# Eight instead of six projection units ahead of the recurrence, and eight instead of ten ahead of the state-space part

## The chip, the cores and the metric

The kernel runs on one core of one Trainium2 chip. A core has five engines that run their own instruction streams and meet through semaphores: TensorE (PE in the rows; PEld is its weight load), VectorE (DVE), ScalarE (ACT), GpSimd (POOL) and SyncE (SP, which here only issues DMAs). The metric is the device time of one execution in microseconds. The kernel before takes 3821.53 us, the median of three runs from 3819.82 to 3821.96.

## The reference, cut to what matters

The program computes two transformer-like blocks in a row. The change lies in the second block, in its mixers. There a normed input h (1024 tokens x 1024 channels) is projected by one wide weight, and four mixers work on slices of the result:

```
h = rmsnorm_2(x, g_mix[l])
u = h @ w_in[l]
c_q, c_kv, k_r, u_pool, z, xbc, dt, lru_g, lru_x, gates = jnp.split(u, pts, axis=-1)
y_a = mla_mixer(...)     # attention
y_b = pool_mixer(u_pool, ...)
y_c = ssd_mixer(z, xbc, dt, ...)     # state-space part: silu(causal conv(xbc)), then chunks
y_d = rglru_mixer(lru_g, lru_x, ...) # recurrence: causal conv, two gates, scan, gelu gate
```

Each mixer needs only its own columns of u; the gates are needed after all four. So the projection can be made piece by piece, in between the mixers' own work.

## The kernel before, in words

`mixers` (L3452) builds one block in which every engine runs one long list: the join of the first block's result (`Join`), then the recurrence (`Recurrence`), the pooling mixer (`Pooling`), the state-space part (`StateSpace`), attention (`Attention`), and what is left of the projection.

The projection (`Projection`, F in the code) has 60 weight tiles of 128 columns, n = 0 to 59, and each tile gives two units, m = 2n and 2n + 1, one for each half of the 1024 tokens. A unit is 24 matmuls of 128x512 (8 steps over the channels, each as three products of split values, lines L100 to L102). Its output bank is one of three, by m modulo 3. Tiles 0 to 7 are, in turn, the x and g parts of the recurrence's four channel groups; 8 to 11 are the pooling's, 12 to 17 the convolution inputs of the state-space part, 18 holds dt and the rotary key, 19 to 22 are z.

A tile takes this way. SP loads it (`load`, L2611). POOL splits it into a high and a low part (`halve`, L2622 and L2624) into one of two buffers. PE makes its two units (`multiply`). ACT copies each unit out of its bank (`take`, L2671), the even unit of a tile only after the store of the tile two before has landed. SP stores the tile to a scratch in HBM (`store`, L2677). The mixer that wants it has SP load it from there (`lr_x`, `lr_g`, `po_u`, `sda_x`).

Nothing is planned by a scheduler: the order on each engine is the order of the calls. `multiply(pe, count)` on PE and `take(act, count)` on ACT make the next `count` units wherever they stand, and both keep a running number, so a call with a larger count shifts every later unit forward. The first three units are made inside the join, so that `multiply(pe, 6)` ahead of the recurrence adds units 3, 4 and 5.

ACT runs `F.take(act, lru.FIRST)` and then `lru.scalar`, whose first work is the exponential and logarithm of a small table sp8 (L2815, L2817). DVE's list of the recurrence waits for those two (`act_own`) before its first convolution (L2723 to L2726, then the bias, L2778). PE's first recurrence matmuls (L2808) wait for that convolution. After them come, for each of four channel groups, 4, 4, 4 and 2 units. Pooling has 4 units first, then one behind each of its four matmul pairs (L2895). The state-space part then has 10 units before its first own work on PE, and two after that.

SP's list is one loop over the tiles. In turn n it issues the load of tile n + 2, the store of tile n, and whatever loads the mixers want of tile n. In turn 12 the state-space part's loads begin, and they begin with a wait for the end of the recurrence and the pooling (L2911 is the pooling's):

```
if n == U_XBC:
    for e in self.earlier:
        e.over(sp)
```

`over` waits until all stores of that mixer have landed. Tile 14 is issued in turn 12 ahead of this wait, tile 15 in turn 13 behind it.

Of the kernel before, what the change touches and what calls it, by code (L numbers as in the profile page):

```python
# [348 lines left out]
class Inputs:  # L349
# [163 lines left out]
    def turn(self, pe, bank, ident):  # L513
        x = self.turns
        i = self.rows[x]
        n, a, m, last = self.pieces[i]
        pe.wait_ge(self.taken, i + 1)
        if x >= 2:
            pe.wait_ge(self.placed, x - 1)
        for c in range(m // P):  # L520
            mm = self.nc.tensor.transpose(bank[:, c * P:(c + 1) * P], self.ob[self.slot[i]][:, c * P:(c + 1) * P], ident)
        mm.then_inc(self.turned, 1)
        self.turns += 1
# [2205 lines left out]
class Recurrence:  # L2729


    FIRST, NEXT = 6, (4, 4, 4, 2)

    def __init__(self, nc, s, q, A, R, F, banks):
        self.nc, self.A, self.R, self.F, self.ps = nc, A, R, F, banks
# [178 lines left out]
class StateSpace:  # L2914
# [114 lines left out]
    def tensor(self, pe):  # L3029
        mm_, ps, C = self.nc.tensor.matmul, self.ps, self.C  # L3030
        turn = self.nc.tensor.transpose
        self.F.multiply(pe, 10)
        for e in self.earlier:
            e.over(pe)
        pe.wait_ge(self.got, 96)
        pe.wait_ge(self.dt_in, 16)
        for c in range(NCK):
            mm = turn(ps[4][:, c * SH:(c + 1) * SH], self.dtr[:, c * P:(c + 1) * P], C["ident"][0:SH, 0:SH])
        mm.then_inc(self.d_turned, 1)
        self.F.multiply(pe, 2)  # L3040
        pe.wait_ge(self.ready, 2)
        mm_(ps[4][:, 0:NCK * SH], self.incl[:], self.a[:].rearrange("p c h -> p (c h)"), start=True, stop=True)
        mm_(ps[4][:, BANK // 2:BANK // 2 + NCK * SH], C["ones"][:], self.a[:].rearrange("p c h -> p (c h)"), start=True, stop=True).then_inc(self.summed, 1)
        pe.wait_ge(self.silu, 6)
        for i in range(NCK):
            if i >= 2:
                pe.wait_ge(self.moved, i - 1)
            for n in range(4):
                turn(ps[i % 2][:, n * P:(n + 1) * P], self.xo[:, n, i * P:(i + 1) * P], C["ident"][:])
            mm = turn(ps[2 + i % 2][:, 0:P], self.xo[:, 4, i * P:(i + 1) * P], C["ident"][:])  # L3050
            mm.then_inc(self.turned, 1)
            if i % 4 == 3:
                self.F.multiply(pe, 1)

        def rows(i):
            r = [slice(0, 64), slice(64, P)]
            mm_(ps[2][:, 0:P], self.xo[r[0], 4, i * P:(i + 1) * P], self.xo[r[0], 5, i * P:(i + 1) * P], start=True, stop=True).then_inc(self.first, 1)
            for h in range(SH):
                mm_(ps[h // 4][:, h % 4 * P:(h % 4 + 1) * P], self.a[:, i, h:h + 1].broadcast_to([P, P]), self.incl[:], start=True, stop=True)
            pe.wait_ge(self.first, i + 1)  # L3060
            mm_(ps[2][:, P:2 * P], self.xo[r[1], 4, i * P:(i + 1) * P], self.xo[r[1], 5, i * P:(i + 1) * P], start=True, stop=True).then_inc(self.rowed, 1)

        pe.wait_ge(self.moved, NCK)
        rows(0)
        for i in range(NCK):
            pe.wait_ge(self.y_done, i)
            pe.wait_ge(self.y_full, i)
            pe.wait_ge(self.xb_done, i + 1)
            r = [slice(0, 64), slice(64, P)]
            mm_(ps[3][:, 0:256], self.xo[r[0], 5, i * P:(i + 1) * P], self.S[r[0], 0:256], start=True, stop=True).then_inc(self.begun, 1)  # L3070
            mm_(ps[4][:], self.bt[:, i], self.xb[i % 2][:], start=True, stop=True).then_inc(self.summed, 1)
            pe.wait_ge(self.begun, i + 1)
            mm_(ps[3][:, 256:512], self.xo[r[1], 5, i * P:(i + 1) * P], self.S[r[1], 256:512], start=True, stop=True).then_inc(self.summed, 1)
            pe.wait_ge(self.masked, 2 * i + 2)
            if i + 1 < NCK:
                rows(i + 1)
            self.F.halves(pe, 1)
            pe.wait_ge(self.y_done, i + 1)
            for h in range(SH):
                mm = mm_(ps[3][:, h * SHD:(h + 1) * SHD], self.M[:, h, :], self.xt[:, i, h * SHD:(h + 1) * SHD], start=True, stop=True)  # L3080
            mm.then_inc(self.summed, 1)
            self.F.halves(pe, 1)
        self.F.settle()
        self.F.multiply(pe, 1)
        pe.wait_ge(self.z_silu, 4)
        for i in range(NCK):
            if i >= 2:
                pe.wait_ge(self.gated, i - 1)
            for n in range(4):
                mm = turn(ps[i % 2][:, n * P:(n + 1) * P], self.z[:, n, i * P:(i + 1) * P], C["ident"][:])  # L3090
            mm.then_inc(self.z_turned, 1)
        self.F.multiply(pe, 3)
        for i in range(NCK):
            pe.wait_ge(self.scaled, i + 1)
            if i >= 2:
                pe.wait_ge(self.o_moved, i - 1)
            for n in range(4):
                mm = turn(ps[2 + i % 2][:, n * P:(n + 1) * P], self.y[:, i, n * P:(n + 1) * P], C["ident"][:])
            mm.then_inc(self.o_turned, 1)
            if i % 4 == 3:  # L3100
                self.F.multiply(pe, 1)

    def scalar(self, act):
        S, ps = self.nc.scalar, self.ps
        for e in self.earlier:
            e.over(act)
        act.wait_ge(self.got, 96)
        for n in range(6):
            self.F.take(act, 1 if n < 2 else 2)
            act.wait_ge(self.convd, n + 1)  # L3110
            S.activation(self.xo[:, n, :], self.xo[:, n, :], ACT.Silu, bias=self.cb[:, n:n + 1]).then_inc(self.silu, 1)
        S.activation(self.al[:], self.al[:], ACT.Exp).then_inc(self.exped, 1)
        act.wait_ge(self.ready, 1)
        S.activation(self.u[:], self.u[:], ACT.Exp).then_inc(self.exped, 1)
        act.wait_ge(self.exped, 2)
        S.activation(self.u[:], self.u[:], ACT.Ln, bias=1.0).then_inc(self.exped, 1)
        self.F.take(act, 2)
        for i in range(NCK):
            act.wait_ge(self.turned, i + 1)
            S.activation(self.xt[:, i], ps[i % 2][:], ACT.Copy)  # L3120
            S.activation(self.bt[:, i], ps[2 + i % 2][:, 0:P], ACT.Copy).then_inc(self.moved, 1)
            if i % 4 == 3:
                self.F.take(act, 1)
        act.wait_ge(self.ready, 3)
        S.activation(self.eacs[:], self.acs[:], ACT.Exp).then_inc(self.exped, 1)
        S.activation(self.back[:], self.back[:], ACT.Exp).then_inc(self.exped, 1)
        S.activation(self.tot[:], self.tot[:], ACT.Exp).then_inc(self.exped, 1)
        for i in range(NCK):
            act.wait_ge(self.lready, i + 1)
            S.activation(self.L[i % 2][:], self.L[i % 2][:], ACT.Exp).then_inc(self.lexped, 1)  # L3130
            if i:
                self.F.take(act, 1)
        self.F.take(act, 1)
        act.wait_ge(self.z_in, 64)
        for n in range(4):
            S.activation(self.z[:, n, :], self.z[:, n, :], ACT.Silu).then_inc(self.z_silu, 1)
        self.F.take(act, 1)
        for i in range(NCK):
            act.wait_ge(self.gated, i + 1)
            S.activation(self.M[:].rearrange("p h t -> p (h t)")[:, i % 2 * BANK:(i % 2 + 1) * BANK], self.y[:, i], ACT.Square, accum_out=self.ms[:, i:i + 1]).then_inc(self.squared, 1)  # L3140
            if i % 2:
                act.wait_ge(self.squared, i + 1)
        self.F.take(act, 3)
        act.wait_ge(self.gated, NCK + 1)
        S.activation(self.ms[:], self.ms[:], ACT.Sqrt).then_inc(self.rooted, 1)
        for i in range(NCK):
            act.wait_ge(self.o_turned, i + 1)
            for n in range(4):
                ins = S.activation(self.yT[:, n, i * P:(i + 1) * P], ps[2 + i % 2][:, n * P:(n + 1) * P], ACT.Copy, scale=self.gn[:, n:n + 1])
            ins.then_inc(self.o_moved, 1)  # L3150
            if i % 4 == 3:
                self.F.take(act, 1)
        act.wait_ge(self.o_moved, NCK)
        act.dma_start(self.R["y"][8:12].rearrange("k p t -> p k t"), self.yT[:, 0:4, :]).then_inc(self.stored, 16)
# [502 lines left out]
class Tail:  # L3657
# [7 lines left out]
    NB, PAIRS, FIRST = 7, 16, 16  # L3665
# [972 lines left out]
```

## Time and profile before

| | |
|---|---|
| median of three runs | 3821.53 us (3819.82 to 3821.96) |
| the profiled execution | 3822.48 us |
| its span | 3820.8 us |
| PE busy | 3473.8 us, 91% |
| DVE busy | 2424.8 us, 63% |
| ACT busy | 1581.6 us, 41% |
| POOL busy | 1121.3 us, 29% |

The span is the time from the first to the last instruction in the profile of one execution; the 1.7 us beside it lie around it. A share is an average over the whole program, and the program has many stages: what an edit does is read from its own stage, which here lies between 1700 and 1960 us of the span.

### The profile page before, as it was taken

Reading aid. Unit: us, or ns where it says so; the run is one execution under the profiler, and the core shown is the slowest. Engines: PE = TensorE matmul, PEld = TensorE weight load, DVE = VectorE, ACT = ScalarE, POOL = GpSimd, SP = SyncE. Lnnn points to the kernel's source line nnn. Section 1 sums busy time; section 2 is a strip of 40 time slices with the busy share of each in tenths; the row PEclk is TensorE's granted clock in tenths of the full one; section 3 lists DMA queues with packets and bytes.
Section 4 is the critical chain, followed back from the end, with each engine's and each line's share of the span. In section 5 each row is a group of like instructions: output and inputs, shape, how many; then the busy total and the mean of one; then the engine's idle time right before and its main releaser. Section 6 shows DMA issues by size and latency. Waiting matters only on the chain. (4 is left out here: it accounts for less than half of the span.)

```text
span 3820.8 us, 44308 instructions
## 1 busy us (share of the span) xinstructions
PE 3473.8 (91%) x16308; PEld 2772.4 (73%) x16308; DVE 2424.8 (63%) x2813; ACT 1581.6 (41%) x2197; POOL 1121.3 (29%) x675
## 2 busy tenths in 40 slices
PE   7899988595999999968989899999889889999997
PEld 3678777464888888846677667777777678878876
DVE  5569557646888888866656222222246488877778
ACT  4322234444777777734221222222232342234444
POOL 1232220135111111143331212222143455545442
PEclk9899999796999999989999999999999999999999
DMA  5312246646899999954421311111153524478854
GB/s 191 110 50 82 104 143 216 223 156 255 354 404 406 404 403 407 393 193 145 156 105 56 127 47 67 59 67 63 55 210 132 190 96 154 153 275 279 266 169 138
DMA packets 225015, 716.70 MB, mean 188 GB/s; under 512 B 26832, under 2 KB 61488, under 8 KB 208720
## 3 DMA queue, kind: packets, MB, share of 16 engines
q1 hardware_dynamic: 184000, 620.37, 44.6%
q10 hardware_dynamic: 31056, 64.28, 4.5%
q0 software_dynamic: 9792, 29.81, 2.0%
q8 instruction: 106, 1.74, 0.2%
q14 instruction: 61, 0.50, 0.0%
HBM read 573.48 MB, written 140.89 MB: 187 GB/s over the span
## 5 line engine op out<-in xcount | busy, mean ns | idle before, releaser
L100 PE MATMUL m_b<-b_high,m_high 128*128 128x512 f32 x960 | 403.5, 420 | 7.7 <-POOL m_low L2624 6.6
L102 PE MATMUL m_b<-b_high,m_low 128*128 128x512 f32 x960 | 377.0, 393 | 0.0
L101 PE MATMUL m_b<-b_rest,m_high 128*128 128x512 f32 x960 | 376.5, 392 | 0.0
L2622 POOL TENSOR_TENSOR m_high<-m_raw,m_one 128x1024 fp32r<-128x1024 f32 x60 | 119.7, 1995 | 759.8 <-PE m_b L102 681.8
L3918 POOL TENSOR_TENSOR t_wl<-t_buf,t_wh 128x512 fp32r<-128x512 f32 x136 | 194.9, 1438 | 240.7 <-ACT t_wh L4049 240.6
L100 PE MATMUL zs_z<-zs_hs,zs_high 128*128 128x512 f32 (+1 forms) x584 | 228.1, 391 | 8.8 <-DVE zs_hs L310 8.3
L2671 ACT ACTIVATE m_ob<-m_b 128x512 f32<-128x512 f32 x120 | 71.0, 596 | 374.3 <-PE m_b L102 338.2
L100 PE MATMUL t_b<-b_high,t_wh 128*128 128x512 f32 x544 | 215.1, 395 | 10.9 <-POOL t_wl L3918 10.9
L100 PEld LDWEIGHTS m_b<-b_high,m_high 128*128 128x128 f32 x960 | 182.2, 190 | 56.0 <-issue 10.2
L101 PE MATMUL zs_z<-zs_hs,zs_high 128*128 128x512 f32 (+1 forms) x584 | 220.3, 377 | 0.0
L102 PE MATMUL zs_z<-zs_hs,zs_low 128*128 128x512 f32 (+1 forms) x584 | 220.3, 377 | 0.0
L101 PEld LDWEIGHTS m_b<-b_rest,m_high 128*128 128x128 f32 x960 | 182.3, 190 | 45.0 <-issue 8.1
L101 PE MATMUL t_b<-b_rest,t_wh 128*128 128x512 f32 x544 | 213.2, 392 | 0.0
L102 PE MATMUL t_b<-b_high,t_wl 128*128 128x512 f32 x544 | 213.0, 391 | 0.0
L2248 DVE TENSOR_TENSOR ex_wlo<-moe_raw,ex_who 128x2048 fp32r<-128x2048 f32 x78 | 178.7, 2293 | 50.4 <-ACT ex_who L2194 49.7
L102 PEld LDWEIGHTS m_b<-b_high,m_low 128*128 128x128 f32 x960 | 181.6, 189 | 39.4
L2248 DVE TENSOR_TENSOR ex_wlg<-ex_raw,ex_whg 128x2048 fp32r<-128x2048 f32 x78 | 178.8, 2293 | 42.0 <-ACT ex_whg L2194 41.8
L4049 ACT ACTIVATE t_wh<-t_buf 128x512 fp32r<-128x512 f32 x136 | 85.8, 631 | 262.0 <-PE t_b L102 77.6
L2248 DVE TENSOR_TENSOR ex_wlu<-moe_raw,ex_whu 128x2048 fp32r<-128x2048 f32 x78 | 178.1, 2284 | 4.0 <-ACT ex_whu L2194 4.0
L428 POOL TENSOR_TENSOR zs_high<-zs_raw,zs_one 128x1024 fp32r<-128x1024 f32 x29 | 58.9, 2030 | 413.7 <-PE zs_z L102 408.5
L3442 DVE TENSOR_SCALAR at_o<-m_b,at_sm 128x64 f32<-128x64 f32 x64 | 18.2, 284 | 228.9 <-PE m_b L3272 201.8
L2194 ACT ACTIVATE ex_whu<-moe_raw 128x2048 fp32r<-128x2048 f32 x78 | 149.4, 1918 | 28.9 <-PE ex_pu L102 26.0
(707 smaller groups left out, 9467.7 us busy)
## 6 DMA issues: line engine op xcount, KB each, us to landing
moe_raw<-in_expert_w SPq DMA_DIRECT2D x79, 2048.0 KB, 10.2
ex_raw<-in_expert_w SPq DMA_DIRECT2D x39, 2048.0 KB, 10.5
t_raw<-in_w_ff SPq DMA_DIRECT2D x192, 256.0 KB, 3.6
m_raw<-in_w_ug SPq DMA_DIRECT2D x60, 512.0 KB, 4.4
t_buf<-hid SPq DMA_DIRECT2D x112, 256.0 KB, 4.4
hid<-t_x SPq DMA_DIRECT2D x96, 256.0 KB, 2.3
yrows<-ex_y ACTq DMA_DIRECT2D x38, 512.0 KB, 10.7
gates<-m_ob SPq DMA_DIRECT2D x32, 512.0 KB, 2.8
```

What stands on the lines that cost most here:

```text
L100: nc.tensor.matmul(out, w[0], x[0], start=first, stop=False)
L101: nc.tensor.matmul(out, w[0], x[1], start=False, stop=False)
L102: return nc.tensor.matmul(out, w[1], x[0], start=False, stop=last)
L428: g.tensor_tensor(self.high[j][:], self.raw[j][:], self.one[:].broadcast_to([P, D]), ALU.mult).then_inc(self.rounded, 1)
L2194: S.activation(half(wh[u], x_), half(raw[slot], x_), ACT.Copy).then_inc(rounded, 1)
L2248: V.tensor_tensor(half(wl[u], x_), half(raw[slot], x_), half(wh[u], x_).bitcast(F32), ALU.subtract).then_inc(left, 1)
L2622: g.tensor_tensor(W.high[j][:], W.raw[j][:], W.one[:].broadcast_to([P, D]), ALU.mult).then_inc(W.rounded, 1)
L2671: self.nc.scalar.activation(self.ob[n % 2][:, c * BANK:(c + 1) * BANK], self.banks[m % len(self.banks)][:], ACT.Copy).then_inc(self.taken, 1)
L3442: V.tensor_scalar(self.o[p % 2][:, b, h % 2 * VH:(h % 2 + 1) * VH], ps[4][:, n % 2 * P:n % 2 * P + VH], sm[:, 1:2], None, ALU.mult).then_i ...
L3918: G.tensor_tensor(self.wl[:, f % 4], self.source(f), self.wh[:, f % 4].bitcast(F32), ALU.subtract).then_inc(self.split, 1)
L4049: S.activation(self.wh[:, f % 4], self.source(f), ACT.Copy).then_inc(self.rounded, 1)
```

## The change

`Recurrence.FIRST` goes from 6 to 8 (PE and ACT both use it), `StateSpace.tensor` multiplies 8 units in front in place of 10, and `StateSpace.scalar` takes one unit ahead of each of its first four activations in place of the first two, so that it takes 8 there in place of 10.

```
-    FIRST, NEXT = 6, (4, 4, 4, 2)
+    FIRST, NEXT = 8, (4, 4, 4, 2)
...
     def tensor(self, pe):
         mm_, ps, C = self.nc.tensor.matmul, self.ps, self.C
         turn = self.nc.tensor.transpose
-        self.F.multiply(pe, 10)
+        self.F.multiply(pe, 8)
...
         for n in range(6):
-            self.F.take(act, 1 if n < 2 else 2)
+            self.F.take(act, 1 if n < 4 else 2)
```

Units 6 and 7 move in front of the recurrence. All units from 8 to 29 are made one place of two earlier in the lists; from unit 30 on each stands where it stood.

## Rows read from the trace of the kernel before

**Rows 1.** Window: length, busy PE, PEld, DVE, ACT, POOL, PE clock, DMA share, GB/s.
```profile
1740.60:1890.00 149.40, 146.80 (x586) 111.46 (x587) 100.58 (x77) 66.50 (x80) 54.25 (x22) 0.97 0.38 139
```

**Rows 2.** Timeline of PE: start, us, instruction, count [idle before, releaser].
```profile
1729.76 0.39 PE L102 MATMUL m_b<-b_high,m_low 128*128 128x512 f32 x1
...
1740.61 3.78 PE L2808 MATMUL m_b<-lr_xc,lr_wa 128*128 128x512 f32 x4 [10.47 <-DVE lr_xc L2778]
...
1871.80 3.43 PE L2895 MATMUL m_b<-po_d,po_w 128*128 128x512 f32 x4 [2.59 <-DVE po_d L2886]
...
1880.55 1.99 PE L2895 MATMUL m_b<-po_d,po_w 128*128 128x512 f32 x4
...
1905.47 0.79 PE L100 MATMUL m_b<-b_high,m_high 128*128 128x512 f32 x1 [6.58 <-POOL m_low L2624]
```

**Rows 3.** Timeline of ACT ahead of the recurrence, and two later takes.
```profile
1730.22 1.09 ACT L2671 ACTIVATE m_ob<-m_b 128x512 f32<-128x512 f32 x2 [10.32 <-DMA u<-m_ob]
...
1734.14 0.20 ACT L2817 ACTIVATE lr_sp<-lr_sp 128x4 f32<-128x4 f32 x1
...
1929.15 0.60 ACT L2671 ACTIVATE m_ob<-m_b 128x512 f32<-128x512 f32 x1 [4.84 <-PE m_b L102]
...
1940.03 0.60 ACT L2671 ACTIVATE m_ob<-m_b 128x512 f32<-128x512 f32 x1 [4.84 <-PE m_b L102]
```

**Rows 4.** Timeline of DVE: the recurrence's first convolution.
```profile
1734.45 0.17 DVE L2770 TENSOR_SCALAR lr_lam<-lr_lam 128x4 f32<-128x4 f32 x1 [5.53 <-ACT lr_sp L2817]
...
1739.81 0.75 DVE L2778 TENSOR_SCALAR lr_xc<-lr_xc,lr_cb 128x1024 f32<-128x1024 f32 x1
```

**Rows 5.** Timeline of SP's DMA issues.
```profile
1735.82 0.32 SPq L2756 DMA_DIRECT2D lr_g<-u  x1
1736.18 0.43 SPq L2611 DMA_DIRECT2D m_raw<-in_w_ug  x1
...
1743.06 0.43 SPq L2611 DMA_DIRECT2D m_raw<-in_w_ug  x1
...
1893.97 0.43 SPq L2611 DMA_DIRECT2D m_raw<-in_w_ug  x1
```

**Rows 6.** Timeline of POOL: splits of tiles 3, 4, 14 and 15.
```profile
1721.41 2.40 POOL L2624 TENSOR_TENSOR m_low<-m_raw,m_high 128x1024 fp32r<-128x1024 f32 x1
1741.51 1.89 POOL L2622 TENSOR_TENSOR m_high<-m_raw,m_one 128x1024 fp32r<-128x1024 f32 x1 [17.70 <-DMA m_raw<-in_w_ug]
...
1869.38 2.12 POOL L2622 TENSOR_TENSOR m_high<-m_raw,m_one 128x1024 fp32r<-128x1024 f32 x1 [10.04 <-PE m_b L102]
...
1900.16 1.98 POOL L2622 TENSOR_TENSOR m_high<-m_raw,m_one 128x1024 fp32r<-128x1024 f32 x1 [26.20 <-DMA m_raw<-in_w_ug]
1902.22 3.20 POOL L2624 TENSOR_TENSOR m_low<-m_raw,m_high 128x1024 fp32r<-128x1024 f32 x1
```

**Rows 7.** Timeline of DVE: steps of pooling and convolutions, beside a split and alone.
```profile
1853.62 0.18 DVE L2885 TENSOR_TENSOR po_d<-lr_x,po_inv 128x16 f32<-128x16 f32 x1
...
1864.75 1.23 DVE L2882 TENSOR_TENSOR lr_x<-po_u 128x1024 f32<-128x1024 f32 x1 [10.74 <-DMA y<-po_d]
...
1869.79 1.75 DVE L2885 TENSOR_TENSOR po_d<-lr_x,po_inv 128x16 f32<-128x16 f32 x1
...
1871.98 3.06 DVE L2882 TENSOR_TENSOR lr_x<-po_u 128x1024 f32<-128x1024 f32 x1 [0.23 <-DMA y<-po_d]
...
1903.25 3.25 DVE L2726 SCALAR_TENSOR_TENSOR sd_xo<-sda_x,sd_cw,sd_xo 128x1024 f32<-128x1024 f32 x1
...
1939.42 1.29 DVE L2726 SCALAR_TENSOR_TENSOR sd_xo<-sda_x,sd_cw,sd_xo 128x1024 f32<-128x1024 f32 x1
```

**Rows 8.** Waits of SP's DMA queue, 1700 to 1960: us in total, times, longest.
```profile
SPq L2911 <- DMA y<-po_d: 20.5, 1, 20.5
```

**Rows 9.** Windows as in rows 1, after the two idle times of PE.
```profile
1744.00:1746.00 2.00, 2.00 (x6) 0.81 (x4) 0.00 (x0) 1.01 (x2) 1.83 (x1) 0.74 0.86 332
...
1908.00:1910.00 2.00, 2.00 (x8) 1.59 (x8) 1.97 (x2) 0.16 (x1) 1.92 (x2) 0.78 0.51 209
```

## The prediction

> **What bounds the kernel now.** I read the busy time by engine first: PE has the largest share, but a share of the whole says nothing of a stage, so I went to windows of the stage that the change touches. Between 1740.6 and 1890 us PE is busy for 146.80 of 149.40 us [rows 1]; the idle time lies ahead of that stretch and behind it. The timeline of PE names the three holes. 10.47 us before the recurrence's first matmuls, ended by DVE's convolution. 2.59 us in pooling, ended by DVE. 6.58 us before 1905.47, ended by POOL's split of a weight tile [rows 2]. So PE's own work bounds the middle, and two chains of other engines bound its two ends. What counts is how the start of unit 30 moves: from there on all lists are as they were, with the same units in the same places, so a shift there reaches the end of the kernel whole.
>
> **The first hole, and what the two units do to it.** Unit 5 ends at 1729.76 + 0.39 = 1730.15 [rows 2]. Units 6 and 7 can follow at once: tile 3 is split by 1721.41 + 2.40 = 1723.8 [rows 6], unit 6's bank was emptied before (ACT's takes of units 0 to 3 lie before the wait in rows 3), and unit 7's bank is free once unit 4 is taken, at about 1730.8 [rows 3]. A unit is (1940.03 - 1929.15) / 2 = 5.44 us [rows 3]. So they run from 1730.15 to 1741.03, in the place of the hole.
>
> But the hole was not free time of the recurrence; it was the time of a chain. ACT takes units 4 and 5 (1730.22, 1.09 for both), then runs the exponential and the logarithm until 1734.34. DVE waits for that, convolves from 1734.45 to 1740.56, and PE goes on at 1740.61 [rows 2 to 4]. From the last take to PE that is 1740.61 - 1731.31 = 9.3 us. In the changed kernel ACT has two more takes ahead of the same chain, and the last needs unit 7. It starts at about 1741.1 and ends at 1741.7, where it ended at 1731.31: +10.4 us. The take of unit 6 also wants the store of tile 1 landed; SP's load of that tile, which waits for the same landing, goes out at 1735.82 [rows 5], 0.2 us after unit 6 is ready (1735.6), and unit 7 covers that. PE's hole is thus moved behind the two units, not filled. Term one: **+10.4**.
>
> **A split that now falls on the convolution.** Tile 4 is loaded at 1736.18 and its split starts when it lands, 1741.51, 5.3 us later. Tile 5 is loaded at 1743.06 [rows 5, 6]. Before, its split had to wait for PE to leave tile 3, until after the recurrence's first matmuls; now PE leaves tile 3 at 1741.03, so the split starts at landing, 1743.06 + 5.3 = 1748.4. The convolution now runs from 1744.9 to 1751.0 and meets it. What a DVE step loses to each of the two POOL instructions stands in rows: beside the subtraction (POOL from 1902.22) a convolution step takes 3.25 us and alone 1.29, so 1.96; beside the multiplication (POOL from 1869.38) a small step takes 1.75 and alone 0.18, so 1.57 [rows 6, 7]. Together 3.5. At 1748.4 the last 2.6 us of the convolution are left, enough for both to come between steps. The bounds are 0 (the tile lands after 1751.0) and 4.3 (DVE stands for both in full, 1.89 and 2.40 us). I take the 3.5 of the rows, as the tile would have to land over 2 us late to miss. Term two: **+3.5**.
>
> The Trainium skill, "SBUF — State Buffer", section "Who interferes with whom", says that DVE and GpSimd hold their shared ports for a whole instruction and that the other then blocks entirely. The step of 3.25 us agrees. By that rule both POOL instructions would stand in front of a DVE step here in full, and the sum would end 0.8 higher.
>
> **The middle.** The recurrence and the first part of pooling keep 14 and 8 units, the same matmuls, and the same order; PE has 97% of a full clock there [rows 1] and hardly a hole, so they cost the same. Scratch loads of the recurrence come a tile earlier, but no PE hole there is put down to one, so I count nothing (bounds -1 and +1: one convolution ends within 1 us of when PE wants it).
>
> In pooling one thing changes. Splits are triggered when PE leaves a tile, so the split at 1869.38 (tile 14) would now be that of tile 15, which is not loaded yet (below). It was in DVE's way: a step of 16 columns took 1.75 in place of 0.18 us, and the next group's first step 3.06 in place of 1.23 [rows 7]. Without it pooling's third matmuls start 1.6 us earlier (1870.2). The fourth wait for DVE, which starts at 1871.98 because of a store, and ends 1.8 us earlier, at 1878.7, in place of 1880.5 [rows 2, 7]. PE is ready about then. Bounds: 0, and 3.3 if the lost clock of the 2.59 us hole came back whole as well. Term three: **-1.8**.
>
> **The last hole, and why nothing comes back there.** The two units taken off the state-space front are units 28 and 29 (tile 14). Before, PE made them from about 1888 to 1898.9, then waited 6.58 us for tile 15 [rows 2]. What holds tile 15 is SP: it stood 20.5 us for pooling's last store [rows 8], then issued six constants, one scratch load, and tile 15 at 1893.97 [rows 5]; landing and split take until 1905.42 [rows 6]. PE finishes pooling at 1888.0, so this chain is 17.5 us long, and nothing in it depends on units 28 and 29. In the changed kernel these two are made inside pooling, PE has nothing to do while the chain runs, and the hole becomes 6.58 + 10.88 = 17.5 us. The 10.9 us of matmuls removed are covered idle time: term four **0**. What costs is the restart: after the hole of 10.47 us the granted clock was still mixed (0.74) 4 to 5 us after PE began, after that of 6.58 us (0.78) only 3 to 4 us [rows 2, 9]. At half rate one more microsecond of it costs half. Term five: **+0.5** (0 to 1.5).
>
> The takes on ACT regroup with the units: two fewer ahead of its silus, each as soon as its unit is done. Later takes and convolutions wait for units 30 to 37, which keep their spacing, so that is 0. SP's store of tile 14 no longer waits for a take; the load behind it goes out earlier and nobody waits for it.
>
> **Sum.** 10.4 + 3.5 - 1.8 + 0 + 0.5 = **+12.6 us**. The profiled execution has 3822.48 (span 3820.8); it would be 3835.1. It lay 0.95 above the median of 3821.53, so the forecast median is **3834.1**. All low ends: 10.4 + 0 - 3.3 + 0 - 1 = +6.1 (3827.6). All high ends: 10.4 + 4.3 + 1.5 + 1 = +17.2 (3838.7). A change can be told from none here from 0.2%, or 7.6 us.
>
> **The rivals.**
>
> The recurrence isn't held up (the units fill the hole). For it: PE rests there, and its matmuls need only DVE. Against it: DVE was itself released by ACT's logarithm [rows 4], which stands behind the takes. If it held, pooling would end as before and tile 15 with it, the last hole would eat the gain, and only term three is left: -1.8, a median of 3819.7.
>
> The other side, faster: the filled hole is kept. That needs the rival above, and that tile 15 doesn't wait for pooling's end. Its place is SP's wait of 20.5 us; it decides as soon as tile 15 is issued 10.9 us earlier relative to the end of pooling. Then -10.5, 3811.0. Against it stands SP's order: the tile went out only behind that wait [rows 5, 8]. The Trainium skill, "Perfetto Trace Analysis", section "Optimization Strategy", advises finding the gaps on the limiting engine and what blocks them, and interleaving stages. Filling the gap by it would give this rival's time; the traced releasers speak against it.
>
> Slower still: the longer wait adds another one, for instance tile 1's store landing after 1741, or a bank not emptied when the shifted units want it, in a stretch where PE has no slack: 2 to 5 us more, 3837 to 3840.
>
> **How the numbers follow.** Forecast 0.77, recurrence not held 0.10, faster 0.05, slower still 0.08. The forecast's lowest corner lies under 7.6 us, which moves 0.02 of it to no change. So slower 0.83, no change 0.12, faster 0.05. The range goes from 3827.5, the low corner, to 3839.0, which takes in about half of the last rival, and leaves out somewhat under 2 in 10.
>
> **What would show it.** In the changed profile: PE's hole before L2808 still 10 to 14 us long, now starting near 1741, with L2808 at about 1754.5. A DVE step of that convolution of 2.5 us or more beside POOL's split of tile 5; without it term two is wrong. Pooling's hole 1 us or less, and no split in it. PE idle for about 17 us before L100, ended by POOL, at about 1918. From there on everything later by one constant amount. The prediction is wrong if L2808 starts near 1741 (first rival), or if the hole before unit 30 stays near 6.6 us (second).

## The result, and the profile after

The changed kernel takes 3835.64 us (median of 7 runs, 3831.27 to 3839.51) against 3821.96 for the kernel before (7 runs). The ratio is 1.0033, 95% interval 1.0022 to 1.0045: slower by 8 to 17 us, 12.6 in the middle. The forecast was +12.6; that the two agree to the tenth is luck, as the interval is 9 us wide and the medians lie 13.7 apart. The change is just clear of the 0.2% that the prediction took as its bound.

Single executions differ by several us, and in the profiles most of that lies ahead of the mixers: the L100 at which PE begins units 1 and 2, behind the join's last transposes, starts anywhere from 1698 to 1706 us. (Unit 0 stands earlier, inside the join, some 30 us before that.) So the steps are compared inside the mixers, from that matmul, here called the first L100, to attention's last transposes (L3230), one profile each. I call this span M. Single profiles scatter too: from L3038, the transposes of dt, to the end of M all kernels of this document have the same work on PE, and their profiles show 802.8 to 804.9 us for it. Timeline of PE before, start and end of M, and L3038:

```profile
1702.70 0.47 PE L100 MATMUL m_b<-b_high,m_high 128*128 128x512 f32 x1 [0.60 <-DVE b_rest L2395]
...
1956.14 0.99 PE L3038 MATMUL m_b<-all_ident,sda_dtr 8*128 8x8 f32 x8 [5.27 <-DMA sda_dtr<-u]
...
2759.19 1.09 PE L3230 MATMUL m_b<-all_ident,at_o 128*128 128x128 f32 x8 [0.45 <-DVE at_o L3442]
```

Timeline of PE after, the same three and what answers to [rows 2]:

```profile
1701.49 0.47 PE L100 MATMUL m_b<-b_high,m_high 128*128 128x512 f32 x1 [0.60 <-DVE b_rest L2395]
...
1739.43 0.39 PE L102 MATMUL m_b<-b_high,m_low 128*128 128x512 f32 x1
...
1753.98 3.78 PE L2808 MATMUL m_b<-lr_xc,lr_wa 128*128 128x512 f32 x4 [14.17 <-DVE lr_xc L2778]
...
1883.69 1.98 PE L2895 MATMUL m_b<-po_d,po_w 128*128 128x512 f32 x4 [1.02 <-DVE po_d L2886]
...
1892.18 1.98 PE L2895 MATMUL m_b<-po_d,po_w 128*128 128x512 f32 x4 [1.01 <-DVE po_d L2886]
...
1917.09 0.80 PE L100 MATMUL m_b<-b_high,m_high 128*128 128x512 f32 x1 [17.44 <-POOL m_low L2624]
...
1968.64 0.99 PE L3038 MATMUL m_b<-all_ident,sda_dtr 8*128 8x8 f32 x8 [5.25 <-DMA sda_dtr<-u]
...
2772.57 1.09 PE L3230 MATMUL m_b<-all_ident,at_o 128*128 128x128 f32 x8 [0.45 <-DVE at_o L3442]
```

M was 2759.19 - 1702.70 = 1056.49 and is 1071.08. Worked out from these rows and [rows 2], each time counted from the first L100 of its own profile:

| | before | after | later by |
|---|---|---|---|
| recurrence's first matmuls, L2808 | 37.91 | 52.49 | 14.58 |
| pooling's third matmuls | 169.10 | 182.20 | 13.10 |
| pooling's fourth | 177.85 | 190.69 | 12.84 |
| unit 30 | 202.77 | 215.60 | 12.83 |
| dt's transposes, L3038 | 253.44 | 267.15 | 13.71 |
| end of M | 1056.49 | 1071.08 | 14.59 |

The whole loss is there at the first line. It shrinks by 1.7 us in pooling, nothing of it returns where two units were taken away, and 1.8 us come back behind unit 30.

The chain ahead of the recurrence, after: ACT, then DVE, then POOL, to be laid beside [rows 3, 4, 6].

```profile
1739.85 0.60 ACT L2671 ACTIVATE m_ob<-m_b 128x512 f32<-128x512 f32 x1 [4.81 <-PE m_b L102]
...
1743.28 0.21 ACT L2817 ACTIVATE lr_sp<-lr_sp 128x4 f32<-128x4 f32 x1
```
```profile
1743.59 0.94 DVE L2770 TENSOR_SCALAR lr_lam<-lr_lam 128x4 f32<-128x4 f32 x1 [16.03 <-ACT lr_sp L2817]
...
1748.39 2.79 DVE L2726 SCALAR_TENSOR_TENSOR lr_xc<-lr_x,lr_cw,lr_xc 128x1024 f32<-128x1024 f32 x1
1751.22 2.71 DVE L2778 TENSOR_SCALAR lr_xc<-lr_xc,lr_cb 128x1024 f32<-128x1024 f32 x1
...
1883.25 0.17 DVE L2885 TENSOR_TENSOR po_d<-lr_x,po_inv 128x16 f32<-128x16 f32 x1
```
```profile
1742.16 2.34 POOL L2624 TENSOR_TENSOR m_low<-m_raw,m_high 128x1024 fp32r<-128x1024 f32 x1
1747.33 2.78 POOL L2622 TENSOR_TENSOR m_high<-m_raw,m_one 128x1024 fp32r<-128x1024 f32 x1 [2.83 <-issue]
1750.18 3.20 POOL L2624 TENSOR_TENSOR m_low<-m_raw,m_high 128x1024 fp32r<-128x1024 f32 x1
...
1911.69 2.07 POOL L2622 TENSOR_TENSOR m_high<-m_raw,m_one 128x1024 fp32r<-128x1024 f32 x1 [38.88 <-DMA m_raw<-in_w_ug]
```

The reader is to see three things. The last take ends at 1740.45 and the logarithm starts 2.8 us later, as before (most of that is two table loads of ACT, 1.28 us each). Tile 5's split (1747.33 to 1753.38) lies across the convolution's last two steps, which take 2.79 and 2.71 us where they took 1.28 and 0.75 (0.75 stands in [rows 4], 1.28 below). And in pooling the 16-column step is back at 0.17 us, as POOL has no tile to split there: it waits 38.88 us for tile 15. The convolution's step before, then SP's wait for pooling's last store after (20.5 us before, [rows 8]), and its issue of tile 15 after:

```profile
1738.48 1.28 DVE L2726 SCALAR_TENSOR_TENSOR lr_xc<-lr_x,lr_cw,lr_xc 128x1024 f32<-128x1024 f32 x1
```

```profile
SPq L2911 <- DMA y<-po_d: 33.1, 1, 33.1
```
```profile
1905.59 0.43 SPq L2611 DMA_DIRECT2D m_raw<-in_w_ug  x1
```

### The profile page after: what moved, and what is told of

It reads as the page before. It is cut to its first block and busy times, and to the rows that moved or that the text cites. A ratio compares the mean times of both kernels' runs of the same rounds, so it can differ in the third digit from the quotient of the medians.

```text
span 3833.9 us, 44308 instructions
## 1 busy us (share of the span) xinstructions
PE 3480.2 (91%) x16308; PEld 2775.8 (72%) x16308; DVE 2424.0 (63%) x2813; ACT 1581.9 (41%) x2197; POOL 1121.3 (29%) x675
## 3 DMA queue, kind: packets, MB, share of 16 engines
q8 instruction: 106, 1.74, 0.2%
## 5 line engine op out<-in xcount | busy, mean ns | idle before, releaser
L100 PE MATMUL m_b<-b_high,m_high 128*128 128x512 f32 x960 | 403.4, 420 | 18.7 <-POOL m_low L2624 17.4
L100 PE MATMUL zs_z<-zs_hs,zs_high 128*128 128x512 f32 (+1 forms) x584 | 226.6, 388 | 8.2 <-DVE zs_hs L310 7.8
L100 PEld LDWEIGHTS m_b<-b_high,m_high 128*128 128x128 f32 x960 | 182.2, 190 | 67.0 <-POOL m_low L2624 17.9
L100 PE MATMUL t_b<-b_high,t_wh 128*128 128x512 f32 x544 | 215.3, 396 | 10.1 <-POOL t_wl L3918 9.9
## 6 DMA issues: line engine op xcount, KB each, us to landing
moe_raw<-in_expert_w SPq DMA_DIRECT2D x79, 2048.0 KB, 10.2
```

What stands on the lines that cost most here:

```text
L100: nc.tensor.matmul(out, w[0], x[0], start=first, stop=False)
```

## The experiments

The theory: two gates. The recurrence stands behind the takes (ACT, then DVE), so the moved units delay it; and the front of the state-space part stands behind SP's wait for pooling's end, so removing units there only uncovers idle time. The main rivals: that the loss is in the shifted tiles and splits, or that pooling's late end binds by itself through the scratch loads, convolutions and silus. Each ratio below is to the kernel before as it was timed along with that run: a median of 3822.93 us for the first four kernels, 3823.98 us for the last four.

In the kernels with edits in the recurrence the line numbers behind it are one higher (L2896 for L2895, L3231 for L3230).

### Takes of units 6 and 7 behind the logarithm

```
-                F.take(act, lru.FIRST)
+                F.take(act, 6)
...
         S.activation(sp8[:], sp8[:], ACT.Ln, bias=1.0).then_inc(self.act_own, 1)
+        self.F.take(act, 2)
```

> The changed kernel, with ACT's takes of units 6 and 7 moved behind the exponential and the logarithm of sp8, PE's order untouched. My theory (the 10.4 us are the chain of ACT and DVE standing behind the two new takes): ACT's logarithm ends about 1734 again, the convolution about 1741, and L2808 follows unit 7 within 1 us, at 1741 to 1742; PE's hole ahead of it is gone. The hole before unit 30 stays at 17 us, because tile 15 still waits for pooling's end, so the time comes back only to that of the kernel before or 1 to 2 us under it: 3820 to 3822. Rival one (the loss is in the shifted tiles and splits, not in this chain): stays at 3834 to 3836. Rival two (filling a hole of PE is worth its length): 3810 to 3812.

Measured: 3819.88 us, ratio to before 0.9991 (0.9981 to 1.0000). M is 1053.93, 17.2 under the changed kernel and 2.6 under before. Timelines of PE and of ACT:

```profile
1705.44 0.47 PE L100 MATMUL m_b<-b_high,m_high 128*128 128x512 f32 x1 [0.60 <-DVE b_rest L2395]
...
1743.61 1.88 PE L2808 MATMUL m_b<-lr_xc,lr_wa 128*128 128x512 f32 x4
...
1905.79 0.80 PE L100 MATMUL m_b<-b_high,m_high 128*128 128x512 f32 x1 [17.46 <-POOL m_low L2624]
...
2759.37 1.09 PE L3231 MATMUL m_b<-all_ident,at_o 128*128 128x128 f32 x8 [0.45 <-DVE at_o L3443]
```
```profile
1736.35 0.21 ACT L2817 ACTIVATE lr_sp<-lr_sp 128x4 f32<-128x4 f32 x1
```

The logarithm starts 30.91 us after the first L100 (31.44 before, 41.79 in the changed kernel). L2808 stands with no idle time in front, 38.17 us after the first L100, as before (37.91), and now with two more units done. The hole before unit 30 is 17.46 us. So ACT's order is the first gate, and the filled hole alone is worth next to nothing: the second gate eats it.

### The split of tile 5 held behind the convolution

```
                 for n in range(2, N_UG):
+                    if n == 5:
+                        pool_.wait_ge(lru.convd, 1)
                     F.halve(pool_, n)
```

> The changed kernel, with POOL's split of tile 5 held until the recurrence's first convolution is done. My theory (the split costs the convolution 3.5 us): its last two steps take 1.28 and 0.75 us again, L2808 starts 3.5 us earlier and everything behind it too: 3832 against 3835.6. Tile 5 is wanted by unit 10, 16 us after L2808 starts, so the hold costs nothing. Rival (the slow steps only stand beside something else that is late, such as the load of the x part): no change, 3835.6.

Measured: 3833.57 us, 1.0027 (1.0016 to 1.0038), an interval that overlaps the changed kernel's; M 1066.48, 4.6 under it. Timelines of PE and of DVE:

```profile
1752.47 3.78 PE L2808 MATMUL m_b<-lr_xc,lr_wa 128*128 128x512 f32 x4 [10.67 <-DVE lr_xc L2778]
```
```profile
1745.58 0.90 DVE L2770 TENSOR_SCALAR lr_lam<-lr_lam 128x4 f32<-128x4 f32 x1 [16.37 <-ACT lr_sp L2817]
...
1750.34 1.28 DVE L2726 SCALAR_TENSOR_TENSOR lr_xc<-lr_x,lr_cw,lr_xc 128x1024 f32<-128x1024 f32 x1
1751.66 0.75 DVE L2778 TENSOR_SCALAR lr_xc<-lr_xc,lr_cb 128x1024 f32<-128x1024 f32 x1
```

The first L100 of this profile is at 1703.48, so L2808 comes at 48.99, 3.50 us earlier than in the changed kernel, and unit 30 still 3.65 us earlier (211.95 in place of 215.60). The split costs those 3.5 us, and only by its timing. That rests on this profile; the medians alone can't tell the two kernels apart.

### Tile 15 ahead of the wait for pooling

```
-                    if n >= 2:
+                    if n >= 2 and n != U_XBC + 1:
                         F.load(sp, n + 2)
+                    if n == U_XBC:
+                        F.load(sp, n + 3)
                     F.store(sp, n)
```

> The changed kernel, with the load of weight tile 15 issued ahead of SP's wait for the end of pooling. My theory (the removal of two units gives nothing because the chain pooling's end, tile 15, split is fixed): PE's hole of 17.4 us before unit 30 disappears, ended within 1 us of unit 29. How much of it reaches the end depends on what is late next: the first scratch load of the state-space part is still behind pooling's end, and ACT takes units 31 to 35 only behind silus, so PE will wait for banks. I expect 8 to 15 us under the changed kernel, 3821 to 3828, with the split of tile 15 back in pooling's way (1.7 us). Rival (the hole is really due to pooling's end through the scratch loads and takes): 3834 to 3836.

Measured: 3836.35 us, 1.0032 (1.0020 to 1.0045). M is 1067.91, only 3.2 under the changed kernel. A miss. Timelines of PE, SP and POOL:

```profile
1928.37 0.80 PE L100 MATMUL m_b<-b_high,m_high 128*128 128x512 f32 x1 [11.79 <-POOL m_low L2624]
```
```profile
1917.71 0.43 SPq L2611 DMA_DIRECT2D m_raw<-in_w_ug  x1
```
```profile
1923.15 1.89 POOL L2622 TENSOR_TENSOR m_high<-m_raw,m_one 128x1024 fp32r<-128x1024 f32 x1 [31.65 <-DMA m_raw<-in_w_ug]
```

The hole before unit 30 is gone, as expected, but one now stands two units later: 11.79 us before unit 32, ended by the split of tile 16, which SP now issues behind the same wait and two scratch loads that go out one after the other (at 1911.24 and 1917.34; the tile at 1917.71). Pooling's hole is back at 2.59 us, with tile 15's split in its place, as expected. My expectation named one load where the gate is all of SP's list behind pooling's end.

### Both

Both diffs above.

> Both edits: the takes of units 6 and 7 behind sp8's two activations, and tile 15 loaded ahead of the wait. My theory (two separate gates, each of which alone gives back only its own hole): the sum of the two gains, 13 from the first and 8 to 15 from the second, 3807 to 3814, clearly under the kernel before. Rival (the state-space part's front is bound by its scratch loads, convolutions and silus, from pooling's end on): no better than the takes alone, 3820 to 3822.

Measured: 3818.46 us, 0.9992 (0.9983 to 1.0000); M 1053.20, hardly under the 1053.93 of the moved takes alone. The same miss: 12.54 us of idle time before unit 32.

```profile
1906.39 0.79 PE L100 MATMUL m_b<-b_high,m_high 128*128 128x512 f32 x1 [12.54 <-POOL m_low L2624]
```

After these four runs two accounts were left: SP's list, or pooling's end itself. Three of the next four kernels move more of SP's list out of the way; the other one (tile 14's split) is a test of term three.

### SP's list reordered, in the kernel before

Ahead of the wait: the loads of tiles 15 and 16 and the store of tile 13.

```
-                    if n >= 2:
+                    if n >= 2 and n != 14:
                         F.load(sp, n + 2)
                     F.store(sp, n)
+                    if n == 13:
+                        F.load(sp, 16)
...
-                    ssd.load(sp, n)
+                    for k in (12, 13) if n == 13 else () if n == 12 else (n,):
+                        ssd.load(sp, k)
```

> The kernel before (6 and 10), with SP's list reordered around the wait for pooling's end: the loads of tiles 15 and 16 and the store of tile 13 are issued ahead of it, the scratch loads of tiles 12 and 13 behind. My theory after the last run (loading tile 15 alone only moves the wait to tile 16; the gate is the whole of SP's list behind pooling's end): PE's 6.6 us hole before unit 30 goes, and no hole of over 3 us stands before unit 32; the mixers, from their first projection matmul to attention's last transposes, take 5 to 8 us less than the 1056.5 of before. Rival (pooling's end binds through the first scratch load, the convolutions and the silus that ACT's takes stand behind): within 2 us of 1056.5.

Measured: 3815.51 us, 0.9979 (0.9970 to 0.9988); M 1050.57, 5.9 under before, inside the 5 to 8 expected. The one hole left in this stretch is 1.49 us, before unit 34:

```profile
1921.97 0.50 PE L100 MATMUL m_b<-b_high,m_high 128*128 128x512 f32 x1 [1.49 <-POOL m_low L2624]
```

### The split of tile 14 held, in the kernel before

```
                 for n in range(2, N_UG):
+                    if n == 14:
+                        pool_.wait_ge(pool.pooled, 4)
                     F.halve(pool_, n)
```

> The kernel before, with POOL's split of tile 14 held until pooling's last DVE work is done. My theory (term three: this split costs pooling's DVE steps 1.6 and then 1.8 us): the step of 16 columns takes 0.2 instead of 1.75 us, PE's hole in pooling falls from 2.6 to 1.0, pooling's fourth matmuls start 1.7 us earlier relative to the second, and unit 30 too, as tile 15's load follows pooling's end; the mixers take 1.5 to 2 us less than 1056.5. Rival (an off-path saving): 1056.5.

Measured: 3822.87 us, 0.9994 (0.9985 to 1.0003), which tells nothing from no change; M 1057.65, 1.2 over before. Timelines of PE and DVE, then windows with the granted clock (the column ahead of the DMA share):

```profile
1703.20 0.47 PE L100 MATMUL m_b<-b_high,m_high 128*128 128x512 f32 x1 [0.60 <-DVE b_rest L2395]
...
1871.18 1.98 PE L2895 MATMUL m_b<-po_d,po_w 128*128 128x512 f32 x4 [1.01 <-DVE po_d L2886]
...
1904.61 0.79 PE L100 MATMUL m_b<-b_high,m_high 128*128 128x512 f32 x1 [6.62 <-POOL m_low L2624]
```
```profile
1870.74 0.17 DVE L2885 TENSOR_TENSOR po_d<-lr_x,po_inv 128x16 f32<-128x16 f32 x1
```
```profile
1908.60:1910.60 2.00, 2.00 (x6) 1.60 (x5) 2.00 (x1) 0.00 (x0) 1.65 (x1) 0.50 0.41 168
1910.60:1912.60 2.00, 2.00 (x10) 1.60 (x10) 1.97 (x2) 0.00 (x0) 0.00 (x0) 1.00 0.71 217
```

The local half is right: the step takes 0.17 us, the hole 1.01, and unit 30 comes 201.41 us after the first L100 in place of 202.77, 1.4 earlier. But the gain was gone again at L3038, 50.67 us after unit 30 before and 51.86 here: in this execution the clock stayed at 0.50 for 6 us after PE had resumed. So the saving exists where it was placed, and this run doesn't show that it reaches the end. The profile of the kernel with the takes moved, which has no split there either, does keep it: against before it is 0.64 us early at pooling's second matmuls, 2.22 at the third (166.88 in place of 169.10), 2.29 at L3038 and 2.56 at the end of M. A saving of this size is near the scatter of single profiles.

### SP's list reordered, in the changed kernel

The loads of tiles 15 and 16 and the stores of tiles 13 and 14 ahead of the wait.

```
-                    ssd.load(sp, n)
+                    for k in (12, 13, 14) if n == 14 else () if n in (12, 13) else (n,):
+                        ssd.load(sp, k)
```

> The changed kernel (8 and 8), with loads of tiles 15 and 16 and stores of tiles 13 and 14 issued ahead of SP's wait for pooling's end, the scratch loads of tiles 12 to 14 behind it. My theory: units 30 to 33 follow pooling at once and the hole of 17.4 us is cut to under 3 at that place; what is late next is tile 17 and the takes behind the silus. The mixers take 1071.1 as changed; I expect 1056 to 1063 here, since the convolutions begin no earlier than before. Rival (the hole is only the sign of pooling's late end, which binds by itself): 1068 to 1071, as with tile 15 alone (1067.9).

Measured: 3823.48 us, 0.9999 (0.9990 to 1.0008); M 1057.19, 13.9 under the changed kernel and inside the 1056 to 1063 expected. One hole of 1.78 us is left, before unit 34, whose tile 17 is the next one late. The hole before the recurrence is still 13.68 us. Pooling's fourth matmuls come at 192.45, later than in the changed kernel (190.69), and M is shorter all the same: pooling's late end doesn't bind by itself.

```profile
1756.61 3.78 PE L2808 MATMUL m_b<-lr_xc,lr_wa 128*128 128x512 f32 x4 [13.68 <-DVE lr_xc L2778]
...
1927.96 0.50 PE L100 MATMUL m_b<-b_high,m_high 128*128 128x512 f32 x1 [1.78 <-POOL m_low L2624]
```

### The takes moved and SP's list reordered

The first diff and the last one together.

> The changed kernel with the takes of units 6 and 7 behind sp8's activations and SP's list reordered around pooling's end. My theory (both gates gone, both holes of PE used): the mixers take 1042 to 1048, 8 to 14 us under the kernel before, and the median is 3809 to 3814. Rival (the state-space front is bound from pooling's end by its own loads, convolutions and silus): 1053 to 1054, as with the takes moved alone.

Measured: 3807.92 us (5 runs), 0.9950 (0.9937 to 0.9964): faster than both kernels. M is 1040.33, 16.2 under before, somewhat better than expected.

```profile
1705.41 0.47 PE L100 MATMUL m_b<-b_high,m_high 128*128 128x512 f32 x1 [0.61 <-DVE b_rest L2395]
...
1743.62 1.89 PE L2808 MATMUL m_b<-lr_xc,lr_wa 128*128 128x512 f32 x4
...
1914.16 0.50 PE L100 MATMUL m_b<-b_high,m_high 128*128 128x512 f32 x1 [1.77 <-POOL m_low L2624]
...
2745.74 1.10 PE L3231 MATMUL m_b<-all_ident,at_o 128*128 128x128 f32 x8 [0.45 <-DVE at_o L3443]
```

What the change is worth depends on the two gates. M in us:

| | 6 and 10 | 8 and 8 | 8 and 8, takes moved |
|---|---|---|---|
| SP's list as it was | 1056.5 | 1071.1 | 1053.9 |
| SP's list reordered | 1050.6 | 1057.2 | 1040.3 |

With both gates open the move of two units saves 10.2 us (1050.57 to 1040.33); with both shut it costs 14.6. (SP's reordered list puts tile 14's store ahead of the wait with 8 and 8 only, so these two kernels differ in that as well.) That the 10.2 is about the length of PE's first hole, 10.28 us in that profile, is in part chance. At L2808 the kernel with both gates open is 0.48 us later for 10.88 us more of units. From there to pooling's second matmuls it gains another 1.27: its clock is 1.00 there, where the other kernel had 0.50 for 6 us behind the hole (L2808's four matmuls take 1.89 us in place of 3.78), and a new hole of 1.52 us takes a part of that back. Then 1.37 go again between pooling's third matmuls and L3038.

## Why the prediction was right

The forecast of 3834.1 lies 1.5 us under the measured median, inside a range of 3827.5 to 3839.0. Its terms, against the two profiles:

**The takes ahead of the chain**, +10.4. ACT's last take ended at 1731.31 and ends at 1740.45, and the mixers began 1.21 us earlier in this profile: +10.35. Moving the takes away removed it. Right, in mechanism and size.

**The split on the convolution**, +3.5. L2808 is 14.58 later, so 4.23 remain. The two steps hit by tile 5's split make 1.51 + 1.96 = 3.5. The other 0.77 is a step of four columns (L2770, 0.94 us in place of 0.17) beside the subtraction of tile 4's split, which I had left out. Holding tile 5 gave 3.50 us back. The reading by which both POOL instructions stand in full, 0.8 us more, didn't come: the steps lost 3.5 and not 4.3. Right, a little under-counted; the prediction's own warning, that the tile would have to land over 2 us late to miss, held: its split began at 1747.33.

**The split no longer in pooling's way**, -1.8. The shift falls from 14.58 to 12.84: -1.74. Right in place and size between those marks; whether it reaches the end is open, as one profile lost it by L3038 (tile 14's split held) and another kept it (takes moved).

**Two units fewer in front of the state-space part**, 0. The hole went from 6.58 to 17.44 us and the shift from 12.84 to 12.83. Right. The reason was too narrow. It named the chain from pooling's end to tile 15; with tile 15 taken out of it, the same list of SP held tile 16.

**The restart**, +0.5. Between unit 30 and L3038 0.88 us were added, but the reason I gave, a longer rest and so a slower restart, fell. It rested on two windows that began at different distances from PE's start, 3.4 and 2.5 us. After rests of nearly the same length the clock came back at different times: in the windows 2 to 4 and 4 to 6 us after unit 30 began the changed kernel (17.44 us of rest) had 0.50 and then 0.68, the one with the takes moved (17.46) 0.57 and then 1.00; after 6.62 us of rest, in the kernel with tile 14's split held, it was at 0.50 for 6 us. Unit 30 to L3038 took 51.55, 50.80 and 51.86 us. Windows of the changed kernel and of the one with the takes moved:

```profile
1919.10:1921.10 2.00, 2.00 (x7) 1.52 (x6) 2.00 (x1) 0.00 (x0) 1.92 (x2) 0.50 0.29 49
1921.10:1923.10 2.00, 2.00 (x8) 1.57 (x7) 1.96 (x2) 0.00 (x0) 2.00 (x1) 0.68 0.84 315
```
```profile
1907.80:1909.80 2.00, 2.00 (x7) 1.58 (x6) 2.00 (x1) 0.00 (x0) 1.92 (x2) 0.57 0.26 53
1909.80:1911.80 2.00, 2.00 (x11) 1.63 (x10) 1.97 (x2) 0.00 (x0) 2.00 (x1) 1.00 0.90 320
```

From L3038 to the end of M another 0.88 us came that no term foresaw. All profiles lie between 802.8 and 804.9 us there (before 803.05, after 803.93), so single profiles don't tell it from chance.

The sum of the terms is 12.6 and M grew by 14.6; the median grew by 13.7. The difference inside M is about 0.7 for tile 4's split, 0.4 more than forecast between unit 30 and L3038, and the 0.9 behind L3038. So the mechanism of the four larger terms held, the reason for the restart didn't, the total came out 2 us under M's, and its nearness to the medians has luck in it. Two of the signs that the prediction named were a little off: the hole before L2808 is 14.17 us, not 10 to 14, and the shift behind unit 30 isn't one constant amount (12.83, then 13.71, then 14.59).

The three rivals. A recurrence that isn't held up is what the kernel with moved takes shows: 3.1 us under before as timed with it, and M 2.6 shorter, where the rival had 1.8. A hole that is kept filled is what the last kernel shows, but the condition that the prediction gave for it, tile 15 issued 10.9 us earlier against pooling's end, was wrong. With both edits tile 15 went ahead of the wait and M was still 1053.20. Only with SP's list reordered did it come to 1040.33, 16.2 under before where the rival had 10.5, as the old hole of 6.58 us went as well. The third, one more wait in the middle, isn't seen: from L2808 to pooling's second matmuls the shift goes from 14.58 to 14.67 us.

## What to carry to other kernels

A hole in one engine is worth filling only if what ends it doesn't stand behind the filling: look at what the releasing engine has queued in front of the releasing instruction, here two copies ahead of two activations on four columns, 10.4 us. Work taken away in front of a wait saves nothing while another queue's in-order list sets the wait's end, and that list has to be cleared as a whole, since taking its first item out only brings up the second. An edit with no value alone can be worth its full length once both ends are free, so it pays to try the gates before dropping it.

## What the runs showed that I had not expected

The time that the granted clock needs to return to 1.00 after a rest isn't set by the rest's length alone: 4 to 6 us after PE resumed it was 0.68 after 17.44 us of rest and 1.00 after 17.46, and after a rest of 6.62 us it was still 0.50 there. A DVE step of four columns (L2770) lost 0.77 us beside a POOL subtraction (0.94 in place of 0.17): it ended at 1744.53 and the subtraction at 1744.50. One of 16 columns lost 1.57 and one of 1024 columns 1.51, both beside a multiplication. So the loss goes by what is left of the POOL instruction, not by the size of the step.

The Trainium skill, "SBUF — State Buffer", section "Who interferes with whom", says that whichever of the two engines issues first holds the shared ports for its whole instruction, and that the other blocks. This trace agrees with it in the step of 0.94 us, and in the steps of 2.79 and 2.71, which end 1.07 and 0.55 us behind the POOL instruction beside them and take 1.28 and 0.75 alone.
